# Expert stage of a two-block layer: the order of the high and low weights' matmuls on TensorE

## The reference

```python
def peer_route(q, sub_keys):
    s1, s2 = scores of the two halves of q against 128 keys each
    v1, i1 = lax.top_k(s1, 16); v2, i2 = lax.top_k(s2, 16)
    vals, pos = lax.top_k((v1[..., :, None] + v2[..., None, :]).reshape(..., 256), 16)
    idx = i1[pos // 16] * 128 + i2[pos % 16]
    return idx, jax.nn.softmax(vals)

def peer_experts(xc, idx, gates, u, v):
    act = jax.nn.gelu(jnp.einsum("chkd,cd->chk", jnp.take(u, idx, axis=0), xc))
    return jnp.einsum("chk,chkd->cd", act * gates, jnp.take(v, idx, axis=0))
```

## Time and profile before

| | |
|---|---|
| time, median of three runs | 1314.05 us |
| time of the profiled execution | 1314.05 us |
| its span, granted TensorE clock | 1312.2 us, 0.995 of full |
| TensorE matmuls busy | 1285.9 us (98%) |
| TensorE weight loads busy | 1124.1 us (86%) |
| VectorE busy | 1029.3 us (78%) |
| ScalarE busy | 808.6 us (62%) |
| GpSimd busy | 441.2 us (34%) |
| expert stage, tile 0's first high to the first tile of `v` | 574 to 967 us of the span |
| L649 (highs; 128 expert tiles and 31 others) | x1272, 324.1 us |
| L654 (lows) | x1272, 177.1 us |

### The profile page before, as it was taken

How to read it: one execution, slowest core, us unless ns; L and a number is a source line. 1 busy time by engine, 2 the same in 40 slices (tenths; PEclk the granted TensorE clock), 3 DMA queues, 4 the chain that set the end, 5 groups by cost and what they waited for, 6 DMA issues and landing times.

```text
span 1312.2 us, 22781 instructions
## 1 busy us (share of the span) xinstructions
PE 1285.9 (98%) x7580; PEld 1124.1 (86%) x7580; DVE 1029.3 (78%) x2015; ACT 808.6 (62%) x1553; POOL 441.2 (34%) x255
## 2 busy tenths in 40 slices
PE   7999999999999999999999999999999999999997
PEld 7998988888877997998888888888888888888886
DVE  4777658557676985689996889898746899999996
ACT  6546446445566446455657888888756566666664
POOL 2100505000022754038888777777750000000000
PEclk9989999999999999999999999999999999999999
DMA  8533126555554533545555544554466655655553
GB/s 306 174 99 113 49 95 198 190 191 189 191 160 144 175 130 129 177 153 187 189 179 187 164 161 161 161 161 161 161 194 224 223 200 201 204 198 192 194 191 112
DMA packets 64652, 225.38 MB, mean 172 GB/s; under 512 B 7201, under 2 KB 7713, under 8 KB 64177
## 3 DMA queue, kind: packets, MB, share of 16 engines
q1 hardware_dynamic: 62832, 218.36, 50.4%
q10 hardware_dynamic: 1728, 5.84, 1.3%
HBM read 223.12 MB, written 1.05 MB: 171 GB/s over the span
## 4 chain that ended last, share of the span: by engine, by line
PE 84%; DVE 11%; issue 2%; ACT 1%; POOL 0%; ACTq 0%; POOLq 0%; DVEq 0%
PE bank L634 41%; PE bank L649 17%; PE bank L654 9%; PE bank L1193 2%; PE bank L1220 2%; PE bank L1221 2%; PE bank L1224 2%; DVE arena L2516 1%; DVE arena L2519 1%; DVE arena L2518 1%; DVE bank L2498 1%; DVE w_lo L1983 1%; DVE arena L2517 1%; PE bank L750 1%; PE bank L898 1%
## 5 line engine op out<-in xcount | busy, mean ns | idle before, releaser
L1331 ACT ACTIVATE w_hi<-ring 128x1024 fp32r<-128x1024 f32 x380 | 402.1, 1058 | 342.7 <-issue 169.0
L1983 DVE TENSOR_TENSOR w_lo<-ring,w_hi 128x1024 fp32r<-128x1024 f32 x225 | 275.0, 1223 | 143.0 <-ACT w_hi L1331 138.2
L1935 POOL TENSOR_TENSOR w_lo<-ring,w_hi 128x1024 fp32r<-128x1024 f32 x128 | 308.0, 2408 | 142.1 <-ACT w_hi L1331 142.1
L649 PE MATMUL bank<-hT,w_hi 128*128 128x512 f32 x1272 | 324.1, 396 | 1.9 <-ACT arena L1673 1.9
L649 PEld LDWEIGHTS bank<-hT,w_hi 128*128 128x128 f32 x1272 | 228.2, 189 | 43.2 <-ACT arena L1673 2.3
L1832 POOL TENSOR_SCALAR mstat<-mstat 128x1 f32<-128x1 f32 x16 | 5.8, 361 | 535.9 <-ACT bank L1288 334.2
L654 PEld LDWEIGHTS bank<-hT,w_lo 128*128 128x128 f32 x1272 | 173.5, 190 | 12.7
L654 PE MATMUL bank<-hT,w_lo 128*128 128x256 f32 x1272 | 177.1, 282 | 0.0
L634 PE MATMUL bank<-w_hi,wgt_hi 128*128 128x512 f32 x368 | 143.4, 390 | 0.1
L634 PE MATMUL bank<-w_hi,wgt_lo 128*128 128x512 f32 x368 | 143.2, 389 | 0.0
L634 PE MATMUL bank<-hT,w_hi 128*128 128x256 f32 (+2 forms) x848 | 113.6, 287 | 0.0
(11 more groups left out here) (397 smaller groups left out, 2191.7 us busy)
## 6 DMA issues: line engine op xcount, KB each, us to landing
ring<-in_stream SPq DMA_DIRECT2D x380, 512.0 KB, 3.5
arena<-in_stream SPq DMA_DIRECT2D x34, 512.0 KB, 4.5
arena<-in_rows ACTq DMA_DIRECT2D x1, 1536.0 KB, 11.2
consts<-in_consts ACTq DMA_DIRECT2D x1, 1152.0 KB, 6.2
arena<-in_keys ACTq DMA_DIRECT2D x1, 1024.0 KB, 4.8
h<-in_x SPq DMA_DIRECT2D x2, 256.0 KB, 4.0
h<-in_x ACTq DMA_DIRECT2D x2, 256.0 KB, 4.1
arena<-in_rows ACTq DMA_DIRECT2D x1, 512.0 KB, 4.0
```

Source lines behind the costliest of these rows:

```text
L649: mm = nc.tensor.matmul(both, w_hi[:, slot, k * P:(k + 1) * P], x_both[:, k, :, :], start=k == 0, stop=False)
L1331: nc.scalar.activation(w_hi[:, g % S, :], ring[:, g % R, :], ACT.Copy).then_inc(hi_done, 1)
L1935: nc.gpsimd.tensor_tensor(w_lo[:, g % S, :], ring[:, g % R, :], w_hi[:, g % S, :].bitcast(F32), ALU.subtract).then_inc(lo_done, 1)
L1983: nc.vector.tensor_tensor(w_lo[:, g % S, :], ring[:, g % R, :], w_hi[:, g % S, :].bitcast(F32), ALU.subtract).then_inc(lo_done, 1)
```

## The change

TensorE's work is shifted by half a tile. The highs of tile 0 stand alone; then each period alternates, matmul by matmul, a high of tile e + 1 with a low of tile e, in two banks (`up_pair`); the lows of tile 127 stand alone. A period starts when the low split of tile e, the high split of tile e + 1, and the gelu (from tile 56 also the late gating) of the tile that had the bank of e + 1 are all there. ScalarE's high splits go one tile further ahead, and the gelu of tiles up to 51 is taken one turn earlier (lag 1 everywhere).

```diff
 def gelu_lag(e):
 
-    return 0 if e not in WIDE else 2 if e < PAIRED else 1
+    return 1
...
+            def up_pair(b_low, low, b_high, high):
+
+                (low_slot, low_done), (high_slot, _) = low, high
+                pe.wait_ge(lo_done, low_done)
+                for k in range(KD):
+                    part = slice(k * P, (k + 1) * P)
+                    mm_high = nc.tensor.matmul(bank[b_high][:, :], w_hi[:, high_slot, part], x_both[:, k, :, :],
+                                               start=k == 0, stop=False)
+                    mm_low = nc.tensor.matmul(bank[b_low][:, 0:T], w_lo[:, low_slot, part], x_hi[:, k, :],
+                                              start=False, stop=k == KD - 1)
+                mm_high.then_inc(hi_used, 1)
+                mm_low.then_inc(tiles_done, 1)
...
+            def expert_tile(e):
+
+                now = ((G_PEER + e) % S, G_PEER + e + 1)
+                if e + 1 == N_KEYS:
+                    expert_low(now, 4 + e % 4)
+                    return
+                after = tile(G_PEER + e + 1)
+                pe.wait_ge(gel_out, e + 2)
+                if e + 1 >= PAIRED + 4:
+                    pe.wait_ge(late_out, e + 1 - PAIRED - 3)
+                up_pair(4 + e % 4, now, 4 + (e + 1) % 4, after)
+
+            w = tile(G_PEER)
+            pe.wait_ge(gel_out, 1)
+            expert_high(w, 4)
+            for e in range(PEER_BODY - 1):
+                expert_tile(e)
+            with pe.Fori(0, ROUTED // PEER_BODY - 1) as i:
                 for j in range(PEER_BODY):
-                    g = G_PEER + j
-                    pe.wait_ge(hi_done, i * PEER_BODY + (g + 1))
-
-                    pe.wait_ge(gel_out, i * PEER_BODY + j + 1)
-                    up_block((g % S, i * PEER_BODY + (g + 1)), 4 + j)
+                    g = G_PEER + PEER_BODY - 1 + j
+                    pe.wait_ge(hi_done, i * PEER_BODY + (g + 2))
+
+                    pe.wait_ge(gel_out, i * PEER_BODY + (PEER_BODY + j + 1))
+                    up_pair(4 + (j + 3) % 4, (g % S, i * PEER_BODY + (g + 1)), 4 + j, ((g + 1) % S, 0))
...
-                        hi(g + S, i, PEER_BODY)
-                        act.wait_ge(up_out, i * PEER_BODY + (up_out_u + j - 1))
-                        nc.scalar.activation(act_all[:, bass.ds(i * PEER_BODY + (j - 2), 1), :].rearrange("p a t -> p (a t)"),
-                                             bank[4 + (j + 2) % 4][:, 0:T], ACT.Gelu_apprx_tanh).then_inc(gel_out, 1)
+                        hi(g + S + 1, i, PEER_BODY)
+                        act.wait_ge(up_out, i * PEER_BODY + (up_out_u + j))
+                        nc.scalar.activation(act_all[:, bass.ds(i * PEER_BODY + (j - 1), 1), :].rearrange("p a t -> p (a t)"),
+                                             bank[4 + (j + 3) % 4][:, 0:T], ACT.Gelu_apprx_tanh).then_inc(gel_out, 1)
...
             def gelu_turn(e):
 
-                hi(G_PEER + e + S)
+                if e + 1 < N_KEYS:
+                    hi(G_PEER + e + S + 1)
                 gelus(e - gelu_lag(e))
```

More of the change, by code:

```diff
@@ L1160, in _, with expert_high @@
             key_scores(NHH // 2 - 1)
-            with pe.Fori(0, ROUTED // PEER_BODY) as i:
-                for j in range(PEER_BODY):
-                    g = G_PEER + j
-                    pe.wait_ge(hi_done, i * PEER_BODY + (g + 1))
-                    pe.wait_ge(gel_out, i * PEER_BODY + j + 1)
-                    up_block((g % S, i * PEER_BODY + (g + 1)), 4 + j)
[L1171 to L1180, removed]
+            def expert_high(w, b):
+                for k in range(KD):
+                    mm = nc.tensor.matmul(bank[b][:, :], w_hi[:, w[0], k * P:(k + 1) * P], x_both[:, k, :, :],
+                                          start=k == 0, stop=False)
+                mm.then_inc(hi_used, 1)
@@ new lines, in expert_low @@
+            def expert_low(w, b):
+                pe.wait_ge(lo_done, w[1])
+                for k in range(KD):
+                    mm = nc.tensor.matmul(bank[b][:, 0:T], w_lo[:, w[0], k * P:(k + 1) * P], x_hi[:, k, :],
+                                          start=False, stop=k == KD - 1)
+                mm.then_inc(tiles_done, 1)
+            def expert_tile(e):
[8 more added lines that the diff above has]
+                up_pair(4 + e % 4, now, 4 + (e + 1) % 4, after)
@@ L1195, in gate_group @@
                 mm.then_inc(g_full, 1)
-            for e in range(ROUTED, PAIRED - 2):
+            for e in range(ROUTED - 1, PAIRED - 2):
                 expert_tile(e)
@@ L1670, in gelu_rounds @@
                         g = G_PEER + j
-                        hi(g + S, i, PEER_BODY)
-                        act.wait_ge(up_out, i * PEER_BODY + (up_out_u + j - 1))
-                        nc.scalar.activation(act_all[:, bass.ds(i * PEER_BODY + (j - 2), 1), :].rearrange("p a t -> p (a t)"),
-                                             bank[4 + (j + 2) % 4][:, 0:T], ACT.Gelu_apprx_tanh).then_inc(gel_out, 1)
+                        hi(g + S + 1, i, PEER_BODY)
+                        act.wait_ge(up_out, i * PEER_BODY + (up_out_u + j))
+                        nc.scalar.activation(act_all[:, bass.ds(i * PEER_BODY + (j - 1), 1), :].rearrange("p a t -> p (a t)"),
+                                             bank[4 + (j + 3) % 4][:, 0:T], ACT.Gelu_apprx_tanh).then_inc(gel_out, 1)
                         act.wait_ge(tiles_done, i * PEER_BODY + (g + 1))
                         nc.scalar.activation(up_u[:, j % 2, :], bank[4 + j][:, T:2 * T], ACT.Copy).then_inc(up_low, 1)
+            hi(G_PEER + S)
             for e in range(PEER_BODY):
-                hi(G_PEER + e + S)
-                if e >= 2:
-                    gelu_split(e - 2, 0)
+                hi(G_PEER + e + S + 1)
+                if e:
+                    gelu_split(e - 1, 0)
                 up_copy(e)
@@ L1686, in _ @@
             gelu_rounds(U_EXP // PEER_BODY, ROUTED // PEER_BODY)
-            next_gelu = [ROUTED - 2]
+            next_gelu = [ROUTED - 1]
             def gelus(last):
```

## The result

| | before | after |
|---|---|---|
| time, median | 1314.13 us (4 runs) | 1323.53 us (4 runs) |
| time of the profiled execution | 1314.05 us | 1323.76 us |
| its span, granted TensorE clock | 1312.2 us, 0.995 | 1322.0 us, 0.993 |

The ratio is 1.0073, with a 95% interval of 1.0061 to 1.0085: slower by 9.4 us. The forecast was +4.7 us and 1312.5 to 1322.5: the sign was right, the size half of what came, and the time lies outside the range.

What follows compares the result with a forecast made beforehand. The prediction took TensorE to bound the kernel, other engines' waits counting only once they reach it. Waits +5.35, pace -0.8 and splits +0.2 gave +4.7 us on 1314.05: 1318.7 us, 8-in-10 range 1312.5 to 1322.5.

Steps and rivals of the forecast that it cites:

- The waits, +5.35 by hand: TensorE's waits for late gelus near tiles 36, 43 and 47 would put it 5.35 us behind by tile 47.
- "Behind": How much later a high starts than before, counting 0.95 us for the low now behind the wait: 2.4 at tile 43.
- The chain by hand: Add times followed through ScalarE's order, VectorE's work unchanged: add 33 at 676.0, pair 42/43 until 698.1, pair 46/47 at 712.2.
- The sign that I had named: Evidence if right: TensorE's waits near tiles 36, 43 and 47, released by gelus, sum to 7 to 10 us.
- The pace, -0.01 us a tile, -0.8 in all: Alternating highs and lows on TensorE would save 0.01 us per tile, counted over 81 tiles: -0.8 us.
- The upper bound that I had drawn from the 272-column matmuls: If 5.3 ns were paid on all sixteen matmuls, a tile would take 2.80 us, +0.01.
- The splits, +0.2: GpSimd's low split, 2.6 to 2.7 of 2.78 us with noticing, is covered by under 0.2; cost +0.2 us in all.
- Gated tiles, 0: ScalarE's gate rows in the gated tiles are done at 2.98, needed at 3.20: cover 0.2 us, cost 0.
- The third rival: Tight covers fail: splits and gate rows reach TensorE late in most tiles, +6 us on top, 1325; chance 0.12.
- Exit, 0: Low 127 standing alone at the stage's end adds no work: cost 0.
- The first rival: The alternation pays: each of 81 tiles saves 0.07 us, -5.7 in all, giving 1313.7 or 1311.0; chance 0.27 together.
- the second: The waits hardly show: VectorE's routing work finds slack, +1 to +2 us less 0.8, 1315; chance 0.12.

Runs made afterwards that it cites:

- e9_ring3: Kernel before, with ScalarE's gelu(n-2) ahead of the high split and TensorE waiting for gelu(n-3) instead of gelu(n-4), both up to tile 51: 1319.41 us.
- its control: Kernel before, with only ScalarE's gelu(n-2) moved ahead of the high split up to tile 51, TensorE's deadline as it was: 1316.39 us.
- e2_lag1: Kernel before, with ScalarE doing the gelu of tile n-1 in turn n in place of tile n-2; TensorE unchanged: 1320.63 us.
- e1_blocks: Changed kernel, but inside each pair eight highs run first and then eight lows, without alternation: 1322.24 us.
- e8_blocks_wait: e1_blocks with the wait on the low split moved behind the eight highs, ahead of the lows: 1322.56 us.
- m1_pace: Matmuls alone, not a whole kernel, in six orders without waits between them: 2.79 us a tile in blocks and two by two, 2.83 one by one.
- e6_exit: Changed kernel, with the last pair taken apart into low 126, then high 127, then low 127: 1324.23 us.
- e5_lag2: Changed kernel, with ScalarE doing gelu(n-2) ahead of the high split in turn n up to tile 51: 1323.39 us.
- e3_exp44: Changed kernel, with ScalarE's softmax exponential four turns later (44 in place of 40): 1323.64 us.
- e13_tail: Changed kernel, with gelu(125) and copy(126) ahead of the high split in ScalarE's turn 126: 1323.52 us.
- e4_lead2: Changed kernel, with highs leading lows by two inside a pair and the low-split wait behind the first two highs: 1322.38 us.
- e7_all: Changed kernel with the edits of e5_lag2, e6_exit and e4_lead2 at once: 1320.43 us.
- e12_two: Changed kernel, but inside a pair two highs and two lows follow each other in place of one and one: 1322.28 us.

## Why the prediction was half right

**The waits, +5.35 by hand: right in place, 0.8 short.** TensorE waited for gelus at pairs 35/36, 42/43 and 46/47, as forecast. "Behind", in the forecast's sense, is the table's number plus 0.95: 3.16 at tile 43 (2.4 forecast) and 6.18 at tile 47 (5.35). The chain by hand was sound: from add 31 to tile 47 it gives 4.4 us, and seven runs show 4.6. Its premise, "with VectorE's work unchanged", was not: add 31 was already 0.62 late, 0.46 of it from the subtraction that GpSimd's split held up, and add 33 was at 676.64 where I had 676.0. The sign that I had named, waits that sum to 7 to 10 us, did not fit my own sum; they are 3.9. The mechanism was not fully named either. I charged the pair only with the 0.95 us of a low that stands behind a wait. It also ends low n 1.84 us later, so that its gelu must follow within 5.6 us in place of 8.4. e9_ring3 against its control shows that this costs 2 us or more by itself (3.0 between the medians). e2_lag1 shows that ScalarE's order costs by itself too (6.5). Together they are more than the 6.2 us by which the changed kernel is behind at tile 47, so they overlap in the same stalls; how the 4.29 us from tile 34 to 47 divide between them isn't shown.

**The pace, -0.01 us a tile, -0.8 in all: this step failed, in sign.** "An alternation gives every low a long matmul before it" and so the rows would come nearer to the pace per column: measured, the alternation costs 18 ns a tile behind tile 47 (1.4 us), and 36 ns by itself. The upper bound that I had drawn from the 272-column matmuls, 2.80 us a tile, is the mean of the stage, and the order by itself passed it (2.83). From -0.8 to +1.4 this is the largest miss.

**The splits, +0.2: too small, twice over.** I gave GpSimd 0.2 to 0.3 us to notice a low's end and got 2.6 to 2.7 of 2.78, covered. In tiles 3 to 29 a split starts 0.36 to 0.43 us behind the start of the last low, which is those 0.2 to 0.3 behind its end; but I left out that TensorE needs another 0.13 to 0.26, in most of these tiles, from the split's end to the pair's first high. With that the round is 2.85, and not covered. In tiles 1 to 34 this is most of the 2.08 of drift; it cost little in the end, the 0.35 by which VectorE came late to add 30, since the stalls from tile 35 on follow VectorE. Where it counts, between tiles 47 and 127, e1_blocks less e8_blocks_wait puts it at 1.03 - 0.40 = 0.6.

**Gated tiles, 0: right.** With the alternation gone the lag doesn't grow from tile 52 to 117 (3.91 to 3.76 in e1_blocks). The cover of the gate rows, 0.2 us by the forecast, held. The third rival came true only for the splits, and mostly ahead of tile 34.

**Exit, 0: wrong by 1.1.** No work was added, but the work behind the last pair moved. I had looked at TensorE's work there and not at the turns of ScalarE behind it.

The forecast was half of what came because one term had the wrong sign and three were too small; none of the four made up for another. Together: 0.8 on the waits, 2.2 on the pace, 0.4 on the splits and 1.1 on the exit make 4.5 of the 5.0 us by which the profiled execution (+9.7) missed the forecast (+4.7); the rest is in the tiles from 47 on and isn't placed. The first rival (the alternation pays) is refuted by m1_pace, the second (the waits hardly show) by the stalls.

## What to carry to other kernels

When two steps of a pipeline are merged into one block, work out for every buffer how long it is held and how long its reader has until the next writer, before and after. Here four banks stayed four banks, but low n ended 1.84 us later and the next writer came 0.95 earlier, so copy, add and gelu had 5.6 us in place of 8.4. Changes upstream of a stall that another engine's fixed order sets are worth nothing: seven runs came to tile 34 between 2.18 us ahead of the kernel before and 1.09 behind it, and all started tile 47 4.6 us behind their add 31. Before two runs are compared, look whether the same instruction takes the same time in both: one subtraction of 0.41 us took up to 2.60, and that shifts a comparison by 2 us. And if matmuls of two lengths are to alternate, measure the order by itself first: ten tiles of each order took one run and would have turned the sign of that term.

## What the runs showed of the hardware

**A half clock that cost nothing where a stall followed.** Behind the wait at pair 42/43 (2.4 us between two starts, 2.1 idle) the changed kernel ran some matmuls at half the rate, 512 columns in 0.42 us:

```profile
700.36 0.62 PE L664 MATMUL bank<-hT,w_hi 128*128 128x512 f32 x1
700.78 0.41 PE L666 MATMUL bank<-hT,w_lo 128*128 128x256 f32 x1
701.00 0.63 PE L664 MATMUL bank<-hT,w_hi 128*128 128x512 f32 x1
```

The windows of the changed kernel there, then those of e6_exit, whose code is the same up to tile 125 (start:end, length, busy and matmuls, granted clock, DMA share, GB/s):

```profile
699.00:703.50 4.50, 4.50 (x18) 0.65 0.46 149
704.00:711.70 7.70, 7.70 (x46) 1.00 0.43 132
```

```profile
699.00:703.50 4.50, 4.47 (x25) 1.00 0.41 150
704.00:711.70 7.70, 6.82 (x38) 1.00 0.42 140
```

Granted 0.65 is a mix of the 1.2 and the 2.4 GHz level; e6_exit, with the same 2.4 us between two starts before it, was granted the full clock. It did 25 matmuls where the changed kernel did 18, and gave the lead back at once, idle in the next stretch. At tile 47 the two are level (5.23 and 5.40). Where no wait for a gelu follows, the loss stays: 1.56 us from tile 42 to 43 in e5_lag2. The half clock stood behind the stalls of after, e1_blocks, e5_lag2, e3_exp44, e8_blocks_wait (twice) and e13_tail, and not behind those, 2.1 to 2.6 us between two starts, of e4_lead2, e6_exit, e7_all and e12_two. What decides it I can't tell from these runs.

**Two rhythms of one order.** The same sequence of instructions ran at 347 ns a high and low in one stretch and 354 in another. In m1_pace it never left the slow one; two by two it never entered it.
